# Second attention: the values of all eight heads of a block in one visit, ten buffers for turned weights, and the reciprocals' rows made by transposes

## The reference, cut to what matters

```python
def mixer_window_attention(q, k, v, gate, sink, bias, mask):
    bsz, seq, _ = q.shape
    nblk = seq // BLOCK
    q = q.reshape(bsz, nblk, BLOCK, N_KV_HEADS, GQA_GROUP, HEAD_DIM)
    ...
    kb, vb = band(k), band(v)
    s = jnp.einsum('bnqkgd,bnskd->bnkgqs', q, kb).astype(jnp.float32) * (HEAD_DIM ** -0.5)
    s = jnp.where(mask[None, :, None, None], s + bias, NEG_INF)
    sk = sink.astype(jnp.float32).reshape(1, 1, N_KV_HEADS, GQA_GROUP, 1, 1)
    m = jnp.maximum(jnp.max(s, axis=-1, keepdims=True), sk)
    p = jnp.exp(s - m)
    p = p / (jnp.sum(p, axis=-1, keepdims=True) + jnp.exp(sk - m))
    o = jnp.einsum('bnkgqs,bnskd->bnqkgd', p.astype(vb.dtype), vb)
    return o.reshape(bsz, seq, W_C) * jax.nn.silu(gate)
```

## Time and profile before

| what | value |
|---|---|
| median of 3 timed runs | 1676.22 us (1675.51 to 1676.41) |
| span of the profiled execution | 1673.8 us |
| timed median less that span (what lies around it) | 2.4 us |
| PE busy | 1628.5 us, 97% of the span |
| DVE busy | 1150.5 us, 69% |
| ACT busy | 623.2 us, 37% |
| POOL busy | 710.5 us, 42% |
| second attention, first scores of block 2 to last values of block 7 | 1484 to 1558 us |

### The profile page before, as it was taken

How to read it: one execution, slowest core, us unless ns; L and a number is a source line. 1 busy time by engine, 2 the same in 40 slices (tenths; PEclk the granted TensorE clock), 3 DMA queues, 4 the chain that set the end, 5 groups by cost and what they waited for, 6 DMA issues and landing times.

```text
span 1673.8 us, 21585 instructions
## 1 busy us (share of the span) xinstructions
PE 1628.5 (97%) x7862; PEld 1331.6 (80%) x7862; DVE 1150.5 (69%) x1702; ACT 623.2 (37%) x980; POOL 710.5 (42%) x390
## 2 busy tenths in 40 slices
PE   9999999999999999999999999999989999999997
PEld 6888787888877888888887778887858888878775
DVE  7231799972498777777767756886965993497456
ACT  6041334421164444444443222264561112268214
POOL 2443211145515233332326687753465555442552
PEclk9999999999999999999999999999999999999999
DMA  5511010123423444334459986331101111110012
GB/s 194 86 39 51 25 39 26 39 72 142 162 114 116 178 159 151 139 143 160 154 184 348 401 336 251 114 142 60 51 13 51 50 41 49 56 45 1 27 37 101
DMA packets 54455, 190.27 MB, mean 114 GB/s; under 512 B 5793, under 2 KB 7730, under 8 KB 53722
## 3 DMA queue, kind: packets, MB, share of 16 engines
q1 hardware_dynamic: 49250, 171.61, 28.3%
q10 hardware_dynamic: 5112, 17.44, 3.6%
HBM read 133.97 MB, written 55.05 MB: 113 GB/s over the span
## 4 chain that ended last, share of the span: by engine, by line
PE 52%; DVE 7%; DMA 3%; issue 2%; POOL 2%; SPq 1%; ACT 1%; ACTq 0%; POOLq 0%; DVEq 0%
PE G L788 16%; PE U L1035 10%; PE G L1035 10%; PE U L1073 4%; PE G L1073 4%; PE G L1109 2%; PE U L1279 1%; SPq L504 1%; PE G L1268 1%; DMA hid_spill<-hst 1%; DMA raw<-in_weights 1%; DMA fraw<-in_weights 1%; PE G L1192 1%; DVE h L2342 1%; DMA hid_spill<-hst_last 1%
## 5 line engine op out<-in xcount | busy, mean ns | idle before, releaser
L611 POOL TENSOR_SCALAR w_hi<-raw 128x1024 fp32r<-128x1024 f32 x50 | 149.4, 2988 | 286.1 <-PE G L788 214.2
L788 PE MATMUL G<-B_hi,w_hi 128*128 128x512 f32 x512 | 159.7, 393 | 3.3 <-DVE B_lo L1963 2.4
L788 PE MATMUL G<-B_lo,w_hi 128*128 128x512 f32 x512 | 157.7, 389 | 0.0
L788 PE MATMUL G<-B_hi,w_lo 128*128 128x512 f32 x512 | 157.6, 389 | 0.0
L788 PE MATMUL G<-A_hi,w_hi 128*128 128x512 f32 x448 | 144.3, 403 | 0.3 <-DVE w_lo L1976 0.3
L654 POOL TENSOR_TENSOR S<-fraw 128x512 f32<-128x512 f32 x33 | 47.2, 1430 | 222.0 <-DVE ring_lo L2237 195.1
L788 PE MATMUL G<-A_lo,w_hi 128*128 128x512 f32 x448 | 139.3, 392 | 0.0
L788 PE MATMUL G<-A_hi,w_lo 128*128 128x512 f32 x448 | 138.6, 391 | 0.0
L613 POOL TENSOR_TENSOR w_lo<-raw,w_hi 128x1024 fp32r<-128x1024 f32 x50 | 132.8, 2655 | 4.2
L1035 PE MATMUL G<-X_lo,ring_hi 128*128 128x512 f32 x308 | 120.3, 391 | 2.2 <-DVE X_lo L2232 2.2
L1035 PE MATMUL G<-X_hi,ring_hi 128*128 128x512 f32 x308 | 120.1, 390 | 1.7 <-DVE ring_lo L2237 1.2
(11 more groups left out here) (395 smaller groups left out, 3788.8 us busy)
## 6 DMA issues: line engine op xcount, KB each, us to landing
raw<-in_weights SPq DMA_DIRECT2D x72, 512.0 KB, 3.6
hid_spill<-hst SPq DMA_DIRECT2D x72, 512.0 KB, 2.6
fraw<-in_weights SPq DMA_DIRECT2D x66, 512.0 KB, 4.5
Dc<-hid_spill SPq DMA_DIRECT2D x56, 512.0 KB, 12.9
Dc<-hid_spill ACTq DMA_DIRECT2D x14, 512.0 KB, 8.0
h<-in_x_t SPq DMA_DIRECT2D x8, 512.0 KB, 7.8
h_spill<-h SPq DMA_DIRECT2D x8, 512.0 KB, 6.7
pj_spill<-pj_out SPq DMA_DIRECT2D x8, 512.0 KB, 2.9
```

What stands on the lines that cost most here:

```text
L611: pool.tensor_scalar(hi, raw[:, u, :], 1.0, None, ALU.mult).then_inc(w_hi_done, 1)
L788: mm = pe.matmul(G[g][:, b * HT:(b + 1) * HT], w, x[:, k, b * HT:(b + 1) * HT], start=s0, stop=s1)
```

## The change

Three things change, and DVE's and ACT's work stays the same in kind and number.

- `values` now takes all eight heads of a block in one call, and is called once in a block, after head 1 of the next block (for the last block at the end). It waits until all eight heads have been copied. `pv_done` counts blocks now, not pairs.
- `pT` becomes eight buffers, one for each head, and two more (`pT_odd`) for heads 0 and 1 of odd blocks. The copies of heads 2 to 7 wait until the values of the block before are done; those of heads 0 and 1 don't wait for values.
- `inverse_rows` makes its four tiles by transposes, not by matmuls with the identity.

```diff
--- before.py
+++ after.py
@@ -298,7 +298,8 @@
 
         k0_hi, k0_lo = [at(f"k0_hi{g}", kb, [P, BAND], F32R) for g, kb in ((0, 60), (1, 62))], [
             at(f"k0_lo{g}", kb, [P, BAND], F32R) for g, kb in ((0, 30), (1, 14))]
-        pT = at("pT", 104, [P, 4, 3, P])
+        pT = [at(f"pT{e}", kb, [P, 3, P]) for e, kb in enumerate((104, 105.5, 107, 108.5, 116, 117.5, 124, 125.5))]
+        pT_odd = [at(f"pT_odd{e}", 120 + 1.5 * e, [P, 3, P]) for e in range(2)]
 
         spread_inv = at("spread_inv", 110, [P, 4, 2, HD])
         mx, nm, den, es, inv = (at(n, 61.5 + i / 16, [P, 2, HEADS2]) for i, n in enumerate(("mx", "nm", "den", "es", "inv")))
@@ -400,6 +401,10 @@
 
             return sS0[hd // 4][:, hd % 4, :] if isinstance(n, int) and n == 0 else sS[:, par, hd, :]
 
+        def turned_of(par, e):
+
+            return pT_odd[e] if par and e < 2 else pT[e]
+
         def queries_of(n, par):
 
             return qs1 if isinstance(n, int) and n == 1 else qs[par]
@@ -1269,15 +1274,16 @@
                                       scores_of(n, par, head(e))[:, kb * P:(kb + 1) * P], ident[:, :])
                 mm.then_inc(pt_done, 1)
 
-            def values(n, par, j, nkb, kb0):
-
-                pe.wait_ge(pT_done, n * HEADS2 + 2 * j + 2)
-                if j == 0 and n >= 1:
+            def values(n, par, nkb, kb0):
+
+                pe.wait_ge(pT_done, (n + 1) * HEADS2)
+                if n >= 1:
                     pe.wait_ge(yc_done, 2 * n)
-                for kb in range(nkb):
-                    for g in range(2):
-                        mm = pe.matmul(U[HD * g:HD * g + HD, 2 + par, j * P:(j + 1) * P], Vt[:, kb0 + kb, HD * g:HD * g + HD],
-                                       pT[:, (2 * j + g) % 4, kb, :], start=(kb == 0), stop=(kb == nkb - 1))
+                for j in range(4):
+                    for kb in range(nkb):
+                        for g in range(2):
+                            mm = pe.matmul(U[HD * g:HD * g + HD, 2 + par, j * P:(j + 1) * P], Vt[:, kb0 + kb, HD * g:HD * g + HD],
+                                           turned_of(par, 2 * j + g)[:, kb, :], start=(kb == 0), stop=(kb == nkb - 1))
                 mm.then_inc(pv_done, 1)
 
             def inverse_rows(n):
@@ -1285,20 +1291,17 @@
                 pe.wait_ge(inv_done, n + 1)
                 pe.wait_ge(yc_done, 2 * n + 1)
                 for j in range(4):
-                    mm = pe.matmul(U[:, 3 - n % 2, j * P:(j + 1) * P], spread_inv[:, j, :, :].rearrange("p a n -> p (a n)"), ident[:, :],
-                                   start=True, stop=True)
+                    mm = pe.transpose(U[:, 3 - n % 2, j * P:(j + 1) * P], spread_inv[:, j, :, :].rearrange("p a n -> p (a n)"), ident[:, :])
                 mm.then_inc(rows_made, 1)
 
-            def weigh(n, nkb, kb0, width=None, left=None):
+            def weigh(n, nkb, width=None, left=None):
 
                 for e in range(HEADS2):
                     if width:
                         qk(n + 2, n % 2, e, width)
                     turn_weights(n, n % 2, e, nkb)
-                    if e == 1 and left:
-                        values(n - 1, (n - 1) % 2, 3, *left)
-                    if e % 2 and e >= 3:
-                        values(n, n % 2, e // 2 - 1, nkb, kb0)
+                    if e == 1:
+                        values(n - 1, (n - 1) % 2, *left)
                     if e == 6:
                         inverse_rows(n)
 
@@ -1331,15 +1334,13 @@
                     turn_weights(0, 0, e + 2, 2)
                 if e == 0:
                     pe.wait_ge(Vt_done, 1)
-                if e % 2:
-                    values(0, 0, e // 2, 2, 0)
                 if e == 6:
                     inverse_rows(0)
-            weigh(1, 3, 0, BAND)
+            weigh(1, 3, BAND, left=(2, 0))
             for n in range(2, 5):
-                weigh(n, 3, n - 1, BAND, left=(3, n - 2))
-            weigh(5, 3, 4, 2 * P, left=(3, 3)), weigh(6, 3, 5, left=(3, 4)), weigh(7, 2, 6, left=(3, 5))
-            values(7, 1, 3, 2, 6)
+                weigh(n, 3, BAND, left=(3, n - 2))
+            weigh(5, 3, 2 * P, left=(3, 3)), weigh(6, 3, left=(3, 4)), weigh(7, 2, left=(3, 5))
+            values(7, 1, 2, 6)
 
 
             gemm(1, S_OUT2, C_OUT2 // 2, 1, B_hi, B_lo, op=3 * KT + X2)
@@ -1850,18 +1851,18 @@
                 if e == HEADS2 - 1:
                     act.activation(es[:, par, :], es[:, par, :], ACT.Exp).then_inc(es_done, 1)
 
-            def turned_w(n, e, nkb):
+            def turned_w(n, par, e, nkb):
                 act.wait_ge(pt_done, n * HEADS2 + e + 1)
 
-                if not (isinstance(n, int) and n * HEADS2 + e < 4):
-                    act.wait_ge(pv_done, n * 4 + e // 2 - 1)
-                act.activation(pT[:, e % 4, 0:nkb, :].rearrange("p k n -> p (k n)"),
+                if e >= 2 and not (isinstance(n, int) and n == 0):
+                    act.wait_ge(pv_done, n)
+                act.activation(turned_of(par, e)[:, 0:nkb, :].rearrange("p k n -> p (k n)"),
                                G[0][:, e % 2 * HT:e % 2 * HT + nkb * P], ACT.Copy).then_inc(pT_done, 1)
 
             def turned_block(n, par, nkb, width):
 
                 for hd in range(HEADS2):
-                    turned_w(n, hd, nkb)
+                    turned_w(n, par, hd, nkb)
                     if width:
                         exps(n + 1, 1 - par, hd, width)
 
@@ -1870,14 +1871,14 @@
             read(21, cvT[:, :], ACT.Copy)
             for hd in range(HEADS2 // 2, HEADS2):
                 exps(0, 0, hd, 2 * P)
-            turned_w(0, 0, 2)
+            turned_w(0, 0, 0, 2)
             act.wait_ge(cvt_done, 1)
             act.activation(Vt[:, :, :].rearrange("p c n -> p (c n)"), U23, ACT.Copy).then_inc(Vt_done, 1)
-            turned_w(0, 1, 2), turned_w(0, 2, 2)
+            turned_w(0, 0, 1, 2), turned_w(0, 0, 2, 2)
             for hd in range(HEADS2):
                 exps(1, 1, hd, BAND)
                 if hd + 3 < HEADS2:
-                    turned_w(0, hd + 3, 2)
+                    turned_w(0, 0, hd + 3, 2)
             with act.Fori(0, 2) as i:
                 turned_block(2 * i + 1, 1, 3, BAND), turned_block(2 * i + 2, 0, 3, BAND)
             turned_block(5, 1, 3, BAND), turned_block(6, 0, 3, 2 * P)
@@ -2667,7 +2668,7 @@
                 dve.tensor_tensor(g, g, U[:, 3 - par, :].rearrange("p (j n) -> p j n", j=4), ALU.mult).then_inc(yc_done, 1)
 
             def gate(n, par):
-                dve.wait_ge(pv_done, 4 * n + 4)
+                dve.wait_ge(pv_done, n + 1)
                 dve.wait_ge(yc_done, 2 * n + 2)
                 g = cg[:, :, bass.ds(n * P, P)]
                 dve.tensor_tensor(g, g, U[:, 2 + par, :].rearrange("p (j n) -> p j n", j=4), ALU.mult).then_inc(yc_done, 1)
```

## The result

| kernel | median, us | lowest to highest | runs |
|---|---|---|---|
| before | 1675.51 | 1673.48 to 1678.69 | 21 |
| changed | 1677.46 | 1674.01 to 1681.16 | 21 |

The ratio is 1.0013, with a 95% interval of 1.0007 to 1.0019: 1.95 us more. That is clear of noise (1.2 to 3.2 us by the interval) and under the 0.2% that the prediction took as the least it could tell from no change. The forecast was 1677.0. The sum it rested on was +0.8 against the kernel before, and the parts of that sum did not all come as they were worked out.

What follows compares the result with a forecast made beforehand. PE bounded before; with the change, ACT's pace plus its idle time in the visit. T(7) 0.8 us earlier, `gate` 0.98 later behind it, low parts 0.6: 1676.2 + 0.8 = 1677.0 us, range 1673.0 to 1680.5.

Steps and rivals of the forecast that it cites:

- The sum it rested on: Whole kernel: 0.2 us from a later `gate` plus 0.6 for the low parts, 0.8 us later in all.
- What bounds a full block: Full attention blocks: ACT's pace plus its idle time in the visit bounds, 9.61 us where it was 10.36.
- The rival that PE bounds all the way: Attention blocks: PE stays the bound, full blocks take 9.0 us, total 1668.4; chance 0.12.
- The worth of the edits on PE: PE in a block: three visits fewer save 0.93 us, transposed rows save 0.44; about 1.37 less work.
- The rival that transposes are no cheaper: Reciprocals' rows: the 0.44 us comes back in block 1 and once at the end, 1677.9; no separate chance given.
- The sum up to T(7): Attention, blocks 1 to 7: gains of full blocks mostly given back by the last two, 0.8 us earlier.
- T(7): End of ACT's last copy (head 7) of block 7; T(n) is the same for block n. Forecast 0.8 us earlier.
- Behind T(7): After the last copy: `gate` follows by 2.11 us, 0.98 later than before, and low parts lose 0.6.
- the order turned round: After the attention: POOL's split, at about 1558.97, starts ahead of the low part behind the gate, at 1559.06.
- the 0.6: After the attention: us lost by a DVE low part starting amid POOL's first split, within bounds of nothing to 2.0.
- The rival of the ports: After the attention: the low part stands for all of POOL's first split, 2.0 us lost, 1678.4; chance 0.22.
- The rival feared for the attention: One attention block: PE's clock falls from 2.4 to 1.2 GHz, some 8 us more, 1684; chance 0.06.

Runs made afterwards that it cites:

- two_visits: Changed kernel with the merged visit split in two per block and block 7 going pair by pair: 1672.25 us, 0.9983 of the kernel before.
- rows_only: Kernel before with only the reciprocals' rows made by transposes, values staying in four visits: 1672.47 us, 0.9981 of the kernel before.
- tail_pairs: Changed kernel with blocks 6 and 7 back to visits of one pair of heads, merged visit in blocks 0 to 5: 1674.64 us.
- split_late: Changed kernel with POOL's first split behind the attention waiting until DVE has made all eight low parts: 1677.90 us.
- visit_only: Changed kernel with the reciprocals' rows made by matmuls again, values staying in one visit: 1678.18 us.
- before_late: Kernel before with POOL's first split behind the attention waiting until DVE has made all eight low parts: 1677.45 us.
- best: Changed kernel with two visits in blocks 0 to 5, pairs in blocks 6 and 7, and POOL's split put off: 1670.52 us, 0.9973 of the kernel before.
- two_tail: Changed kernel with two visits in blocks 0 to 5 and pairs in 6 and 7, POOL's split not put off: 1670.85 us, 0.9974 of before.

## Why the prediction was right where it was, and where it was not

**What bounds a full block.** Right. A full block takes 9.71, with 9.61 forecast and 9.0 if PE had bounded. ACT waits 1.58 to 1.71 ahead of the copy of head 2 in blocks 2 to 5, where some 1.5 was forecast. `two_visits` shows the cause by its other side: with visits of half the length the wait is 0.86 in two pieces and the block falls to 9.41. The rival that PE bounds all the way is out.

**The worth of the edits on PE.** Right to 0.02: 0.46 for four transposes, 2.77 for a visit with what stands behind it. The rival that transposes are no cheaper is out: `rows_only` alone shows 3.2 us of them.

**The sum up to T(7).** The signs were right and the sizes a little off, all one way. Forecast and measured: T(1) 0.6 and 0.53 earlier; T(1) to T(2) 9.87 and 9.88; a full block 9.61 and 9.71, two of them; T(4) to T(5) 9.5 and 9.59; T(5) to T(6) 8.62 and 8.78; T(6) to T(7) 6.6 and 6.72. Added up this is 0.62: -0.18 where -0.8 was forecast. A piece of it has its row: in blocks 3 and 4 ACT's wait was 1.71, and the sum had 1.57 (4.27 less 2.7).

**Behind T(7).** `gate` came 2.07 behind T(7) (2.11 forecast), the order turned round (1557.86 and 1557.93), and `tail_pairs`, which turns it back, shows that this was nearly all of it (100.17 to the fillers, 100.03 before and 101.19 with the change). The forecast put 0.98 and 0.6 behind T(7), 1.58; measured are 1.16. Here the mechanism was only half named. The low part amid POOL's first split lost 0.82, near the 0.6 that I took and far from the rival's 2.6 in all. The 0.6 was misread: free low parts follow each other at less than their length (two in 2.35 in `split_late`), so the two that took 3.19 in the kernel before had lost 0.84 there, as much as the one in the new order. But PE did not lose `gate`'s delay and that loss as such. It lost them as far as they moved POOL's second split from the low part of k = 4 to that of k = 3 (whichever it meets takes about 3.4): one k-step of PE's, 1.36, less 0.20.

**The rival of the ports.** The Trainium skill, SBUF — State Buffer, Who interferes with whom, would have had the low part stand for all of the first split. The trace agrees for the second split (2.2 lost in the 2.66 of POOL's second instruction) and not for the first (0.82 lost beside 2.77). The rival's 1678.4 came from a mechanism that did not happen, and the measured 1677.46 lies between it and the forecast for another reason.

**The clock.** The rival feared for the attention, where the granted clock stayed at 1.00 in both profiles of the changed kernel (and fell in `split_late`, with the same attention). It fell 101 us behind T(7), at the fillers, and cost 0.96, which no part of the prediction held. The forecast's total came out 0.5 us below the measured time because the terms that were off went both ways: attention +0.6, low parts -0.4, fillers +0.96, and 0.7 the other way since the median of before was 1675.51 in this comparison and the sum stood on 1676.2. So the mechanism of the attention was right, but that the total came within 0.5 us is in good part luck. Against the kernel before, the change cost 1.95 where 0.8 was forecast.

**What stays open.** Why the clock falls at the fillers. PE's waits ahead of them are the same with the fall and without (1.50 and 0.23 us in the kernel before and in the changed one). It fell there in both profiles of the changed kernel, in `visit_only`, `tail_pairs` and `before_late`, and in none of `rows_only`, `two_visits`, `best`, `two_tail`, `split_late` and the kernel before (twice). That `before_late` shows it rules the merged visit out as its sole cause; and the time at which the fillers come does not sort them (1656.4 to 1659.9 with the fall, 1650.6 to 1659.5 without). Whether it holds for a kernel's other executions is not shown either. The mean granted clock of the timed executions speaks for it: 0.9940 over the 21 of the changed kernel, 0.9947, 0.9949 and 0.9945 over those of `visit_only`, `tail_pairs` and `before_late`, and 0.9957 to 0.9963 over those of `rows_only`, `two_visits`, `best` and the kernel before. One such fall is worth about 0.0010, an estimate from the two stretches shown (0.49 and 0.36 of 2 us each, in 1674). But `two_tail` has 0.9948 without the fall in its profile.

## What to carry to other kernels

Joining visits to save an engine's change of form pays only as long as the next engine has work in hand to cover the joined visit. Here it has two heads: with the transposes in all three, a full block takes 9.90 in four visits, 9.41 in two of 1.5 us and 9.71 in one of 2.8 us. And it pays only where the engine with the visits is the bound: in blocks 6 and 7 the joined visits lost time, and only `best` and `two_tail`, which leave them apart there, come ahead of the transposes alone (by 1.35 and 1.30 up to T(7)). Cost each edit of a change against the bound that the others leave behind: the transposes were worth 3.2 us alone and 1.3 beside the merged visit. Where a wait is to be taken away by delaying a third engine, look first for who waits for that engine's result and from when; the wait of 2.35 us that came instead was about as long as those that it removed, and the clock fell behind it in two profiles of three. And hold each variant beside the simplest one that shares its gain, not only beside the kernel before.

## What the runs showed of the hardware that was not expected

- A DVE low part (1.22 us free) that started 0.07 behind POOL's first split instruction took 2.04, and beside POOL's second about 3.4. The second reads two tiles in SBUF, the first one; the runs show the sizes and not the reason.
- A wait of PE of 2.34 to 2.38 us was followed by a clock of 0.64 over 1572 to 1575 in `split_late` (the wait ends at 1572.75) and 0.50 over the same 3 us in `before_late` (it ends at 1570.59), and by 1.00 in `best`, with the same code behind it. A wait of 1.5 us in block 0 was followed by 0.61 in `split_late` and by 1.00 in the changed kernel.
- The ten fillers took 2.50 us at a granted clock of 1.00 and 3.94 to 4.13 where it fell (0.51 in the changed kernel), alike in both profiles of the two kernels that have two.
- The start of the attention moves by over 2 us between executions (first copy at 1479.61 to 1482.43), in code that is the same.
